# Expert weights of a mixture-of-experts stage loaded in rows twice as long, with two tiles accumulating at once

## The chip, the cores and the metric

The kernel runs on one core of one Trainium2 chip. The metric is the device time of one execution in microseconds (us), smaller being better.

## The reference

The reference is a two-layer model on 256 latent and 256 context tokens of width 1024: layer 0 has an mLSTM mixer and a dense SwiGLU, layer 1 an HGRN2 mixer and a mixture of eight SwiGLU experts of hidden width 2816, of which each latent token uses two. The change touches only the experts:

```python
def moe_swiglu(u, w_router, b_router, w_gu, w_down):
    logits = (u @ w_router).astype(F32) + b_router.astype(F32)
    top_val, top_idx = lax.top_k(logits, TOP_K)
    weights = jax.nn.softmax(top_val, axis=-1)
    combine = jnp.einsum('...k,...ke->...e', weights, jax.nn.one_hot(top_idx, N_EXPERTS, dtype=F32))
    out = jnp.zeros(u.shape[:-1] + (w_down.shape[-1],), F32)
    for e in range(N_EXPERTS):
        out = out + combine[..., e:e + 1] * swiglu(u, w_gu[e], w_down[e]).astype(F32)
    return out.astype(u.dtype)
```

`swiglu` splits `u @ w_gu` into a gate half and an up half and returns `(silu(g) * up) @ w_down`. All weights are float32: `w_gu` has 1024 rows of 5632 columns per expert, `w_down` 2816 rows of 1024.

## The kernel before, in words

The stages run one after the other; the last but one is `experts` (line 1754). It works through the eight experts in one loop whose body all engines share. For each expert the up to 128 tokens that chose it are gathered (`gather`, TensorE, into PSUM banks 4 and 5; `take`, VectorE, eight operations), multiplied with the weights, and the result is scattered back by a matmul (`scatter`, banks 6 and 7) and added to `acc` by VectorE (`add`, two operations a half).

The matmuls run in three passes, to keep float32 accuracy: each operand is split into a rounded high part and a low rest, and a product is high x high, high x low and low x high (`three_passes`, lines 1850 to 1852). The weights are split on the fly. A **unit** is one transfer into one of four ring slots (`slot`), and two **pieces** are cut from each unit; an expert has 24 units and 48 pieces. For each piece, ScalarE writes the high part (line 1939), VectorE the low part (line 2002), both into one of three piece buffers (`E_BUFS`), and TensorE multiplies with them and counts `used`. Split p waits until piece p-3 is used. A transfer waits until the low parts of both pieces of the unit four back are made (`low_done`, line 1827 issues it on SyncE's queue).

Pieces 0 to 31 belong to the up projection. Its 2816 columns per side are cut into eight tiles of 352. A unit is one tile of one side, all 1024 rows (eight chunks of 128), in rows of 352 x 4 = 1408 bytes, and its two pieces are the lower and the upper four chunks. Tile t takes pieces 4t to 4t+3: two for the gate side, two for the up side. ScalarE's `silu` follows the gate side, VectorE's `hidden` (line 2026) multiplies after the last piece. Tiles alternate between PSUM banks 0, 1 and 2, 3. The hidden rows are turned in six groups by TensorE (`turn_hidden`, after pieces 15, 19, 23, 27, 33, 35) and split again into `hid_h` and `hid_l` (line 2068).

Pieces 32 to 47 belong to the down projection. Each half of 512 output columns is made in turn: first half 0 (pieces 32 to 39) and then half 1 (40 to 47), each from four units of 6, 5, 6, 5 chunks, so pieces of 3, 3, 3, 2, 3, 3, 3, 2 chunks with rows of 2048 bytes. A half's result is weighted and split by `y_high` (line 1953) and `y_low` (line 2032) and then scattered: half 0 at pieces 39 to 43 of the same expert, half 1 in the first pieces of the next one, where both halves' work on piece buffers goes on beside it.

The engines' hand-written places are given by the piece number p in the loops of `three_passes` with `after(p)`, and of ScalarE and VectorE: in each, `split(it, p + 3)` comes first and the other work after it. The rows of the profile name lines of the kernel before; names as `resid`, `tok` and `ex` are areas used again (`e_silu` lies in `resid`, `acc` in `tok`, the raw list in `ex`).

## Time and profile before

| | |
|---|---|
| runs | 2218.1, 2219.05, 2224.69 us |
| median | 2219.05 us |
| profiled execution, span of the core | 2219.4 us |
| TensorE busy over the span | 1969.2 us (89%) |
| VectorE, ScalarE busy | 1394.1 us (63%), 1112.6 us (50%) |
| expert stage, first matmul of a weight piece to last | 1375 to 2202 us |

The page gives one number for the profiled execution, the span from the first to the last instruction of the core, 2219.4 us. The mean rate of the DMA engines over the whole span is 184 GB/s, in the expert stage it is about 335. Engines: PE is TensorE, PEld its weight loads, DVE VectorE, ACT ScalarE, SP SyncE, whose queue SPq issues the transfers. A row of order of time has the start, the duration, the engine, the line and what is written from what; in brackets stand the idle time before it and what ended it. The drawn duration of a matmul (0.32 or 0.39 us) is longer than the distance to the next, since they are pipelined.

### The profile page before, as it was taken

How to read it: one execution, taken by the hardware profiler on the slowest of the kernel's cores; microseconds unless marked ns; L12 is line 12 of the kernel's file. 1: busy time of each engine (PE TensorE's matmuls, PEld its weight loads, DVE VectorE, ACT ScalarE, POOL GpSimd, SP SyncE). 2: the span in 40 equal slices, each digit the busy share in tenths (PEclk: the TensorE clock that was granted, in tenths of full speed). 3: DMA queues.
4: the chain of work that ended last, by engine and by line, in shares of the span. 5: the costliest groups of instructions: out<-in, count | busy, mean ns of one | idle time of the engine just before them, and what ended most of it. 6: DMA issues, size and time to landing. Idle time of an engine off the chain costs nothing. (4 is left out here: it accounts for less than half of the span.)

```text
span 2219.4 us, 26725 instructions
## 1 busy us (share of the span) xinstructions
PE 1969.2 (89%) x10092; PEld 1615.5 (73%) x10092; DVE 1394.1 (63%) x1531; ACT 1112.6 (50%) x1244; POOL 110.5 (5%) x117
## 2 busy tenths in 40 slices
PE   5979988659999997869996675999999999999996
PEld 1247866548888874248895665989899898989895
DVE  5545234553233336745545844888888888888887
ACT  5433332343232225643234434677777777777765
POOL 1000012000000000000004800000000000000000
PEclk9879999879999998979998786999999999999998
DMA  9612210113232314822240004999999999999994
GB/s 328 233 60 104 76 39 1 38 38 114 76 113 76 114 57 172 310 88 94 76 152 1 1 1 149 323 348 324 345 329 348 325 348 319 354 320 336 335 331 175
DMA packets 254248, 409.11 MB, mean 184 GB/s; under 512 B 6575, under 2 KB 160327, under 8 KB 254055
## 3 DMA queue, kind: packets, MB, share of 16 engines
q1 hardware_dynamic: 254184, 408.23, 52.8%
q8 instruction: 43, 0.70, 0.1%
q14 instruction: 21, 0.17, 0.0%
HBM read 407.16 MB, written 1.05 MB: 184 GB/s over the span
## 5 line engine op out<-in xcount | busy, mean ns | idle before, releaser
L2002 DVE TENSOR_TENSOR w_low<-e_ring,w_high 128x1408 fp32r<-128x1408 f32 (+2 forms) x384 | 617.4, 1622 | 102.6 <-ACT w_high L1939 99.4
L1939 ACT ACTIVATE w_high<-e_ring 128x1408 fp32r<-128x1408 f32 (+2 forms) x384 | 528.7, 1382 | 214.7 <-PE ps L1852 212.2
L1850 PE MATMUL ps<-w_high,list_h 128*128 128x352 f32 x1024 | 338.1, 330 | 17.7 <-DVE w_low L2002 16.3
L1852 PE MATMUL ps<-w_high,list_l 128*128 128x352 f32 x1024 | 330.1, 322 | 0.0
L1851 PE MATMUL ps<-w_low,list_h 128*128 128x352 f32 x1024 | 329.3, 322 | 0.0
L1217 DVE TENSOR_TENSOR fw_low<-ring,fw_high 128x1024 fp32r<-128x1024 f32 x66 | 80.9, 1225 | 233.8 <-ACT fw_high L1183 233.8
L1850 PEld LDWEIGHTS ps<-w_high,list_h 128*128 128x128 f32 x1024 | 192.9, 188 | 26.4 <-DVE w_low L2002 25.5
L1183 ACT ACTIVATE fw_high<-ring 128x1024 fp32r<-128x1024 f32 x66 | 70.0, 1060 | 254.7 <-PE ps L1136 168.1
L1851 PEld LDWEIGHTS ps<-w_low,list_h 128*128 128x128 f32 x1024 | 193.7, 189 | 0.3
L1852 PEld LDWEIGHTS ps<-w_high,list_l 128*128 128x128 f32 x1024 | 192.9, 188 | 0.0
L1850 PE MATMUL ps<-w_high,hid_h 128*128 128x512 f32 x352 | 140.4, 399 | 5.4 <-DVE hid_l L2068 5.4
L1134 PE MATMUL ps<-u_high,fw_high 128*128 128x512 f32 x352 | 137.7, 391 | 6.7 <-DVE fw_low L1217 6.7
L1852 PE MATMUL ps<-w_high,hid_l 128*128 128x512 f32 x352 | 137.5, 391 | 0.0
L1136 PE MATMUL ps<-u_high,fw_low 128*128 128x512 f32 x352 | 137.4, 390 | 0.0
L1135 PE MATMUL ps<-u_low,fw_high 128*128 128x512 f32 x352 | 137.4, 390 | 0.0
L1851 PE MATMUL ps<-w_low,hid_h 128*128 128x512 f32 x352 | 137.3, 390 | 0.0
L387 ACT ACTIVATE u_high<-ring 128x1024 fp32r<-128x1024 f32 x96 | 98.5, 1050 | 65.7 <-PE ps L359 42.5
L419 DVE TENSOR_TENSOR u_low<-ring,u_high 128x1024 fp32r<-128x1024 f32 x96 | 111.5, 1218 | 9.5 <-ACT u_high L387 9.3
L594 DVE TENSOR_TENSOR h_part<-ring,h_part 128x1024 fp32r<-128x1024 f32 x40 | 49.0, 1225 | 79.0 <-ACT h_part L588 78.9
L588 ACT ACTIVATE h_part<-ring 128x1024 fp32r<-128x1024 f32 x40 | 42.3, 1057 | 100.9 <-PE ps L1320 100.9
L358 PE MATMUL ps<-u_high,c_parts 128*4 128x512 f32 x192 | 84.6, 441 | 6.9 <-DVE u_low L419 6.9
L359 PE MATMUL ps<-u_low,c_parts 128*4 128x512 f32 x192 | 85.0, 443 | 0.0
(323 smaller groups left out, 3631.7 us busy)
## 6 DMA issues: line engine op xcount, KB each, us to landing
e_ring<-in_e_w_gu_dram SPq DMA_DIRECT2D x128, 1408.0 KB, 8.0
ring<-in_mod_w_dram SPq DMA_DIRECT2D x24, 2048.0 KB
e_ring<-in_e_w_down_dram SPq DMA_DIRECT2D x32, 1536.0 KB, 7.2
e_ring<-in_e_w_down_dram SPq DMA_DIRECT2D x32, 1280.0 KB, 7.6
ring<-in_f_w_gu_dram SPq DMA_DIRECT2D x22, 1024.0 KB
ring<-in_h_w_in_dram SPq DMA_DIRECT2D x10, 2048.0 KB
ring<-in_m_w_in_dram SPq DMA_DIRECT2D x6, 2048.0 KB
ring<-in_f_w_down_dram SPq DMA_DIRECT2D x5, 2048.0 KB
```

The costliest lines, as they stand in the source:

```text
L358: nc.tensor.matmul(k.ps[0:4, n % 2, :], k.c_parts[:, c, :], part(k.u_high, q)[:, m, :], start=False, stop=False)
L359: last = nc.tensor.matmul(k.ps[0:4, n % 2, :], k.c_parts[:, c, :], part(k.u_low, q)[:, m, :], start=False, stop=(c == KD - 1))
L387: nc.scalar.activation(part(k.u_high, q), raw(n, q), ACT.Copy).then_inc(high_done, 1)
L419: nc.vector.tensor_tensor(part(k.u_low, q), raw(n, q), part(k.u_high, q).bitcast(F32), ALU.subtract).then_inc(low_done, 1)
L1134: nc.tensor.matmul(k.ps[:, bank, :], wh[:, m, :], k.u_high[:, m, :], start=(m == 0), stop=False)
L1135: nc.tensor.matmul(k.ps[:, bank, :], wh[:, m, :], k.u_low[:, m, :], start=False, stop=False)
L1136: last = nc.tensor.matmul(k.ps[:, bank, :], wl[:, m, :], k.u_high[:, m, :], start=False, stop=(m == KD - 1))
L1850: nc.tensor.matmul(out, high[:, f, :], w_high[:, c, :], start=(f == 0), stop=False)
L1851: nc.tensor.matmul(out, high[:, f, :], w_low[:, c, :], start=False, stop=False)
L1852: last = nc.tensor.matmul(out, low[:, f, :], w_high[:, c, :], start=False, stop=(f == total - 1))
L1939: nc.scalar.activation(piece(k.w_high, p), raw(p), ACT.Copy).then_inc(S.high_done, 1)
L2002: nc.vector.tensor_tensor(piece(k.w_low, p), raw(p), piece(k.w_high, p).bitcast(F32), ALU.subtract).then_inc(S.low_done, 1)
```

## The change

It does four things.

1. **Rows of w_gu.** A unit is now four chunks of two neighbouring tiles (704 columns, rows of 2816 bytes) of one side. Its two pieces are tile 2q and tile 2q+1 for the same four chunks. Four units make a pair of tiles: gate side lower chunks, gate side upper, up side lower, up side upper. The piece is read out of the slot with a jump from row to row.
2. **Two tiles at once.** The pieces of the two tiles alternate, so both tiles of a pair accumulate in their own banks and end one piece apart. `silu` moves to p % 8 in (2, 3), `hidden` to p % 8 in (6, 7).
3. **Rows of w_down.** A unit is up to three chunks with all 1024 columns (rows of 4096 bytes), its two pieces are the output halves 0 and 1. There are seven units of three chunks and one of one. Both halves end with the expert.
4. **The halves' results.** `y_high`, `y_low`, `scatter` and `add` of both halves now stand at the start of the next expert: scatters after pieces 3 and 6, adds at p = 4 and 7. After the last expert both are left.

The core of the diff:

```diff
@@ -44,7 +44,8 @@
 E_N = 352
 E_TILES = FFN // E_N
 E_SLOT = 6 * HALF
-E_UNITS = 2 * E_TILES + 2 * 4
+E_PAIR = 2 * E_N
+E_UNITS = 2 * E_TILES + 8
 E_BUFS = 3
 E_PIECE = 3 * HALF
...
-    down_units = [(0, 6), (6, 5), (11, 6), (17, 5)]
-    down_pieces = [x for f, m in down_units for x in ((f, 3), (f + 3, m - 3))]
+    down_units = [(f, min(3, FC - f)) for f in range(0, FC, 3)]
+    assert len(down_units) == 8 and E_TILES % 2 == 0
     def slot(j):
         return k.e_ring[:, (j % E_RING) * E_SLOT:(j % E_RING + 1) * E_SLOT]
...
-    def piece(buffer, p):
-        m, n, _ = piece_shape(p)
-        return buffer[:, (p % E_BUFS) * E_PIECE:(p % E_BUFS) * E_PIECE + m * n].rearrange("p (c n) -> p c n", c=m)
-    def raw(p):
-        m, n, first = piece_shape(p)
-        return slot(p // 2)[:, first:first + m * n].rearrange("p (c n) -> p c n", c=m)
...
-                            t, side = j // 2, j % 2
-                            src = gu[:, side * FFN + t * E_N:side * FFN + (t + 1) * E_N].rearrange("(k p) n -> p k n", p=P)
-                            dst = slot(j)[:, 0:KD * E_N].rearrange("p (k n) -> p k n", k=KD)
+                            pair, side, part = j // 4, j // 2 % 2, j % 2
+                            first = side * FFN + pair * E_PAIR
+                            src = gu[part * GS * P:(part + 1) * GS * P, first:first + E_PAIR].rearrange("(k p) n -> p k n", p=P)
+                            dst = slot(j)[:, 0:GS * E_PAIR].rearrange("p (k n) -> p k n", k=GS)
                         else:
-                            half, (f, m) = (j - Y0) // 4, down_units[(j - Y0) % 4]
-                            src = dn[f * P:(f + m) * P, half * HALF:(half + 1) * HALF].rearrange("(k p) n -> p k n", p=P)
-                            dst = slot(j)[:, 0:m * HALF].rearrange("p (k n) -> p k n", k=m)
+                            f, m = down_units[j - Y0]
+                            src = dn[f * P:(f + m) * P, :].rearrange("(k p) n -> p k n", p=P)
+                            dst = slot(j)[:, 0:m * D].rearrange("p (k n) -> p k n", k=m)
                         need = sp.snap(it * PIECES + (2 * j + 2))
...
-                pe.wait_ge(S.added, adds + 3)
...
                 with pe.Fori(0, EXPERTS) as e:
                     it = ps_ * EXPERTS + e
-                    ys = ps_ * 17 + 2 * e
-                    adds = ps_ * 34 + 4 * e
+                    ys = ps_ * 18 + 2 * e
+                    adds = ps_ * 36 + 4 * e
                     pe.wait_ge(S.list_low, ps_ * 9 + e + 1)
                     def after(p):
                         if p == 3:
-                            scatter(ys + 1, adds, 1)
+                            scatter(ys + 1, adds, 0)
+                        elif p == 6:
+                            scatter(ys + 2, adds + 2, 1)
                         elif p == 11:
                             turn_places(it, adds, e)
                         elif p == 21:
@@ -1905,27 +1906,25 @@
                             gather(ps_ * 9 + e + 1)
                         elif p in HIDDEN_TURNS:
                             turn_hidden(it, HIDDEN_TURNS.index(p))
-                        elif p == 42:
-                            pe.wait_ge(S.hid_low, it * HG + HG)
-                            scatter(ys + 2, adds + 2, 0)
-                    for t in range(E_TILES):
-                        pe.wait_ge(S.hid_done, it * E_TILES + t + 1)
-                        for side in range(2):
-                            for b in range(2):
-                                p = 4 * t + 2 * side + b
-                                three_passes(it, p, k.ps[:, 2 * (t % 2) + side, 0:E_N], k.list_h, k.list_l, b * GS, GS, KD)
-                                after(p)
+                    for j in range(Y0):
+                        pair, side, part = j // 4, j // 2 % 2, j % 2
+                        for b in range(2):
+                            if part == 0:
+                                pe.wait_ge(S.hid_done if side else S.silu_ready, it * E_TILES + 2 * pair + b + 1)
+                            three_passes(it, 2 * j + b, k.ps[:, 2 * b + side, 0:E_N], k.list_h, k.list_l, part * GS, GS, KD)
+                            after(2 * j + b)
                     pe.wait_ge(S.list_made, ps_ * 9 + e + 2)
-                    for half in range(2):
-                        for b, (f, m) in enumerate(down_pieces):
-                            if half == 0:
-                                pe.wait_ge(S.hid_low, it * HG + ((f + m - 1) // 4 + 1))
-                            p = 2 * Y0 + 8 * half + b
+                    for n, (f, m) in enumerate(down_units):
+                        pe.wait_ge(S.hid_low, it * HG + ((f + m - 1) // 4 + 1))
+                        for half in range(2):
+                            p = 2 * (Y0 + n) + half
                             three_passes(it, p, k.ps[:, 4 + half, :], k.hid_h, k.hid_l, f, m, FC)
                             after(p)
-                scatter(ps_ * 17 + 17, ps_ * 34 + 32, 1)
+                scatter(ps_ * 18 + 17, ps_ * 36 + 32, 0)
+                scatter(ps_ * 18 + 18, ps_ * 36 + 34, 1)
...
             def silu(it, t):
-                act.wait_ge(S.used, it * PIECES + (E_BUFS + 4 * t + 2))
+                act.wait_ge(S.used, it * PIECES + (E_BUFS + 8 * (t // 2) + 3 + t % 2))
                 act.wait_ge(S.hid_done, it * E_TILES + (t + 1))
...
+            act.nop().then_inc(S.silu_ready, 2)
             def y_high(pieces, half):
-                act.wait_ge(S.used, pieces + E_BUFS)
+                act.wait_ge(S.used, pieces + E_BUFS - 1 + half)
...
                     act.wait_ge(S.gathered, ps_ * 9 + e + 1)
-                    y_high(it * PIECES, 1)
+                    for half in range(2):
+                        y_high(it * PIECES, half)
...
-                        if p < 2 * Y0 and p % 4 == 1:
-                            silu(it, p // 4)
+                        if p < 2 * Y0 and p % 8 in (2, 3):
+                            silu(it, p // 8 * 2 + p % 2)
...
-                        if p == 39:
-                            act.wait_ge(S.pcopied, it + 1)
-                            y_high(it * PIECES + 40, 0)
-                y_high(ps_ * (EXPERTS * PIECES) + EXPERTS * PIECES, 1)
+                for half in range(2):
+                    y_high(ps_ * (EXPERTS * PIECES) + EXPERTS * PIECES, half)
...
             def hidden(it, t):
-                dve.wait_ge(S.used, it * PIECES + (E_BUFS + 4 * t + 4))
-                dve.wait_ge(S.silu_ready, it * E_TILES + (t + 1))
+                dve.wait_ge(S.used, it * PIECES + (E_BUFS + 8 * (t // 2) + 7 + t % 2))
+                dve.wait_ge(S.silu_ready, it * E_TILES + (t + 3))
...
-                    y_low(ys + 1, 1)
+                    for half in range(2):
+                        y_low(ys + 1 + half, half)
...
-                        if p < 2 * Y0 and p % 4 == 3:
-                            hidden(it, p // 4)
-                        if p == 4:
-                            add(adds, 1)
+                        if p < 2 * Y0 and p % 8 in (6, 7):
+                            hidden(it, p // 8 * 2 + p % 2)
+                        if p in (4, 7):
+                            add(adds + (0 if p == 4 else 2), 0 if p == 4 else 1)
...
-                        if p == 40:
-                            y_low(ys + 2, 0)
-                        if p == 43:
-                            add(adds + 2, 0)
-                y_low(ps_ * 17 + 17, 1)
-                add(ps_ * 34 + 32, 1)
+                for half in range(2):
+                    y_low(ps_ * 18 + 17 + half, half)
+                for half in range(2):
+                    add(ps_ * 36 + 32 + 2 * half, half)
```

Two places of VectorE and one of TensorE show the order. First, TensorE at the end of an expert's loop body (three matmuls a chunk; before, pieces 46 and 47 had three and two chunks, and piece 47 is the last of these rows). Before, the last two chunks:

```order
L1850 MATMUL ps<-w_high,hid_h 128x512
L1851 MATMUL ps<-w_low,hid_h 128x512
L1852 MATMUL ps<-w_high,hid_l 128x512
L1850 MATMUL ps<-w_high,hid_h 128x512
L1851 MATMUL ps<-w_low,hid_h 128x512
L1852 MATMUL ps<-w_high,hid_l 128x512
L1846 REGISTER_ALU
L1850 MATMUL ps<-w_high,hid_h 128x512
L1851 MATMUL ps<-w_low,hid_h 128x512
L1852 MATMUL ps<-w_high,hid_l 128x512
L1850 MATMUL ps<-w_high,hid_h 128x512
L1851 MATMUL ps<-w_low,hid_h 128x512
L1852 MATMUL ps<-w_high,hid_l 128x512
```

and with the change, pieces 46 and 47:

```order
L1849 MATMUL ps<-w_high,hid_h 128x512
L1850 MATMUL ps<-w_low,hid_h 128x512
L1851 MATMUL ps<-w_high,hid_l 128x512
L1845 REGISTER_ALU
L1849 MATMUL ps<-w_high,hid_h 128x512
L1850 MATMUL ps<-w_low,hid_h 128x512
L1851 MATMUL ps<-w_high,hid_l 128x512
```

The last two pieces have shrunk from fifteen matmuls to six.

Second, VectorE between split 25 and split 26 (`ex<-ps` is `take`, `e_hid` the hidden product). Before:

```order
L2002 TENSOR_TENSOR w_low<-e_ring,w_high 128x1408
L2013 ISA
L2015 TENSOR_SCALAR ex<-ps,mod_scale,mod_cols 128x128 x8
L2001 REGISTER_ALU
L2002 TENSOR_TENSOR w_low<-e_ring,w_high 128x1408
L2025 REGISTER_ALU
L2026 TENSOR_TENSOR e_hid<-resid,ps 128x352
```

and with the change:

```order
L2002 TENSOR_TENSOR w_low<-e_ring,w_high 128x1408
L2025 REGISTER_ALU
L2026 TENSOR_TENSOR e_hid<-resid,ps 128x352
L2013 ISA
L2015 TENSOR_SCALAR ex<-ps,mod_scale,mod_cols 128x128 x8
L2001 REGISTER_ALU
L2002 TENSOR_TENSOR w_low<-e_ring,w_high 128x1408
L2025 REGISTER_ALU
L2026 TENSOR_TENSOR e_hid<-resid,ps 128x352
```

Hidden product 4 now follows split 25, ahead of `take`, and product 5 follows split 26.

Third, VectorE from its hidden product 0 on (`tok<-tok,ps` is `add`). Before:

```order
L2026 TENSOR_TENSOR e_hid<-resid,ps 128x352
L2001 REGISTER_ALU
L2002 TENSOR_TENSOR w_low<-e_ring,w_high 128x1408
L2037 ISA
L2039 TENSOR_TENSOR tok<-tok,ps 128x512
L2037 REGISTER_ALU
L2039 TENSOR_TENSOR tok<-tok,ps 128x512
L2001 REGISTER_ALU
```

and with the change, from split 9's hidden product on:

```order
L2026 TENSOR_TENSOR e_hid<-resid,ps 128x352
L2001 REGISTER_ALU
L2002 TENSOR_TENSOR w_low<-e_ring,w_high 128x1408
L2025 REGISTER_ALU
L2026 TENSOR_TENSOR e_hid<-resid,ps 128x352
L2037 REGISTER_ALU
L2039 TENSOR_TENSOR tok<-tok,ps 128x512
L2037 REGISTER_ALU
L2039 TENSOR_TENSOR tok<-tok,ps 128x512
L2001 REGISTER_ALU
```

The hidden products come after splits 9 and 10, and a second pair of adds stands between split 10 and split 11.

## Rows read from the trace of the kernel before

**Rows 1.** busy time in one stretch, the fourth expert from first to next first matmul (columns as shown).
```profile
core 0: us, PE busy (x) PEld busy (x) DVE busy (x) ACT busy (x) POOL busy (x), PEclk, DMA share, GB/s
1686.36:1789.47 103.11, 101.24 (x584) 93.68 (x584) 90.69 (x79) 76.50 (x70) 0.00 (x0) 1.00 0.97 335
```

**Rows 2.** waits of that same expert: who waited for whom, us, times, longest.
```profile
ACT w_high L1939 <- PE ps L1852: 26.6, 37, 3.8
PEld ps L1850 <- DVE w_low L2002: 3.7, 5, 1.3
```

**Rows 3.** the page's list of transfers, then order of time: SyncE's issue and ScalarE's use.
```profile
e_ring<-in_e_w_gu_dram SPq DMA_DIRECT2D x128, 1408.0 KB, 8.0
...
1783.14 0.37 SPq L1827 DMA_DIRECT2D e_ring<-in_e_w_gu_dram  x1
...
1793.60 1.38 ACT L1939 ACTIVATE w_high<-e_ring 128x1408 fp32r<-128x1408 f32 x1 [0.52 <-PE ps L1852]
```

**Rows 4.** groups by line and shape, 1400 to 2150: busy us, mean ns.
```profile
L2002 DVE TENSOR_TENSOR w_low<-e_ring,w_high 128x1408 fp32r<-128x1408 f32 x237 | 381.6, 1622 | 66.1 <-ACT w_high L1939 64.4
...
L2002 DVE TENSOR_TENSOR w_low<-e_ring,w_high 128x1024 fp32r<-128x1024 f32 x28 | 34.1, 1217 | 0.0
...
L2068 DVE TENSOR_TENSOR hid_l<-ps,hid_h 128x512 fp32r<-128x512 f32 x37 | 25.3, 683 | 0.0
```

**Rows 5.** order of time where one expert ends and the next begins (start us, us).
```profile
1785.09 1.28 ACT L1939 ACT_TABLE_LOAD   x1
1786.38 1.38 ACT L1939 ACTIVATE w_high<-e_ring 128x1408 fp32r<-128x1408 f32 x1
...
1791.69 1.38 ACT L1939 ACTIVATE w_high<-e_ring 128x1408 fp32r<-128x1408 f32 x1 [0.29 <-PE ps L1852]
...
1787.80 4.86 DVE L2002 TENSOR_TENSOR w_low<-e_ring,w_high 128x1408 fp32r<-128x1408 f32 x3 [0.22 <-ACT w_high L1939]
...
1785.61 0.39 PE L1852 MATMUL ps<-w_high,hid_l 128*128 128x512 f32 x1
...
1789.01 0.39 PE L1852 MATMUL ps<-w_high,hid_l 128*128 128x512 f32 x1
1789.47 0.43 PE L1850 MATMUL ps<-w_high,list_h 128*128 128x352 f32 x1
...
1791.33 0.32 PE L1852 MATMUL ps<-w_high,list_l 128*128 128x352 f32 x1
...
1793.24 0.32 PE L1852 MATMUL ps<-w_high,list_l 128*128 128x352 f32 x1
```

**Rows 6.** order of time around piece 26 of the fourth expert, VectorE and TensorE.
```profile
1740.13 2.63 DVE L2015 TENSOR_SCALAR ex<-ps,mod_scale,mod_cols 128x128 f32<-128x128 f32 x8
1742.68 1.61 DVE L2002 TENSOR_TENSOR w_low<-e_ring,w_high 128x1408 fp32r<-128x1408 f32 x1
1744.22 0.51 DVE L2026 TENSOR_TENSOR e_hid<-resid,ps 128x352 f32<-128x352 f32 x1
...
1744.35 0.43 PE L1850 MATMUL ps<-w_high,list_h 128*128 128x352 f32 x1 [1.03 <-DVE w_low L2002]
```

**Rows 7.** order of time after the last piece of the last expert.
```profile
2201.63 0.39 PE L1852 MATMUL ps<-w_high,hid_l 128*128 128x512 f32 x1
2202.06 0.69 ACT L1953 ACTIVATE ey_high<-ps,ex 128x512 fp32r<-128x512 f32 x1 [4.37 <-PE ps L1852]
...
2204.43 1.28 DVE L2039 TENSOR_TENSOR tok<-tok,ps 128x512 f32<-128x512 f32 x2 [0.90 <-PE ps L1861]
```

**Rows 8.** line 594: duration in ns, min/median/max.
```profile
L594 DVE TENSOR_TENSOR m_part<-ring,m_part x24: 1206/1226/1227, 137.7 to 279.4; 128x1024 fp32r<-128x1024 f32 x24
```

**Rows 9.** order of time, TensorE at piece 8 of the fifth expert.
```profile
1805.66 0.32 PE L1852 MATMUL ps<-w_high,list_l 128*128 128x352 f32 x1
1806.08 0.43 PE L1850 MATMUL ps<-w_high,list_h 128*128 128x352 f32 x1
```

**Rows 10.** order of time, TensorE at piece 37 of the fourth expert.
```profile
1767.55 0.49 PE L1850 MATMUL ps<-w_high,hid_h 128*128 128x512 f32 x1 [0.67 <-DVE hid_l L2068]
```

More of the change, by code:

```diff
@@ L1778, in experts @@
     assert len(HIDDEN_TURNS) == HG
[L1781 to L1782 removed]
+    down_units = [(f, min(3, FC - f)) for f in range(0, FC, 3)]
+    assert len(down_units) == 8 and E_TILES % 2 == 0
     def slot(j):
         return k.e_ring[:, (j % E_RING) * E_SLOT:(j % E_RING + 1) * E_SLOT]
[L1787 to L1792 removed]
     def piece(buffer, p):
[L1795 removed]
+        m, n = (GS, E_N) if p < 2 * Y0 else (down_units[p // 2 - Y0][1], HALF)
         return buffer[:, (p % E_BUFS) * E_PIECE:(p % E_BUFS) * E_PIECE + m * n].rearrange("p (c n) -> p c n", c=m)
     def raw(p):
[L1799 to L1800 removed]
+        b = p % 2
+        if p < 2 * Y0:
+            return slot(p // 2)[:, 0:GS * E_PAIR].rearrange("p (c n) -> p c n", c=GS)[:, :, b * E_N:(b + 1) * E_N]
+        m = down_units[p // 2 - Y0][1]
+        return slot(p // 2)[:, 0:m * D].rearrange("p (c n) -> p c n", c=m)[:, :, b * HALF:(b + 1) * HALF]
     def passes(engine):
@@ L1865, in turn_places @@
             def turn_places(it, adds, e):
-                pe.wait_ge(S.added, adds + 3)
+                pe.wait_ge(S.added, adds + 5)
                 for i in range(2):
@@ L1956, in _ @@
             with act.Fori(0, n) as ps_:
-                act.wait_ge(S.scattered, ps_ * 34 + 1)
+                act.wait_ge(S.scattered, ps_ * 36 + 1)
                 nc.scalar.activation(k.place_cols[:, :], k.slot_no[:, :], ACT.Copy, scale=0.0)
@@ L2046, in _ @@
                     it = ps_ * EXPERTS + e
-                    ys, adds = ps_ * 17 + 2 * e, ps_ * 34 + 4 * e
+                    ys, adds = ps_ * 18 + 2 * e, ps_ * 36 + 4 * e
                     for p in range(E_BUFS):
                         split(it, p)
-                    y_low(ys + 1, 1)
+                    for half in range(2):
+                        y_low(ys + 1 + half, half)
                     for p in range(PIECES):
```

5 lines of the change are left out of this document (removed).

## The prediction

> **What bounds the kernel now.** I read the stretches first, then who waits for whom, then the order of time at the places where TensorE stands still. The change touches only the expert stage, so one expert is the unit: its 48 pieces take 103.1 us from the first matmul of one expert to that of the next, and TensorE is busy for 101.2 of them at the full clock [rows 1]. The same row has the DMA engines at a share of 0.97, VectorE at 90.7 us and ScalarE at 76.5. So two resources look full, and the question is which of them the other waits for. The list of waits answers it: ScalarE, which is the reader of what DMA brings, waited 26.6 us for TensorE to give a buffer back, and no wait for a transfer is listed at all; TensorE waited five times for VectorE's low half, 3.7 us of its weight queue [rows 2]. The DMA engines are kept busy because a transfer starts as soon as a ring slot is free, but it ends early: the transfer for pieces 4 and 5 of one expert was issued at 1783.14, a landing takes 8.0 us as the median, which is 1791.1, and ScalarE started piece 4 at 1793.60, 2.5 us later [rows 3]. **TensorE's own work bounds the stage, plus a few short stalls**, and what the transfers cost is hidden. A change of row length can pay only if it shortens those stalls; a change of order can add some.
>
> Names for the working: split p is the pair ScalarE (high) and VectorE (low) that prepares piece p; there are three piece buffers, so split p may start only when piece p-3 is used. L(p) is the start of the last matmul of piece p.
>
> **Prices.** A ScalarE copy of 1408 columns takes 1.38 us, VectorE's subtraction 1.62; one of 512 columns is taken as the 0.68 of hid_l on VectorE and a little under that on ScalarE [rows 4]. When VectorE has the next job ready it starts it 1.54 after the start of a 1408 split (1742.68 to 1744.22), so 0.08 before its end; likewise 0.43 after the start of a hidden product of 0.51, and 0.60 after the first of two adds (1.28 for two, less 0.68) [rows 5 to 7]. A piece of twelve matmuls of 352 columns costs TensorE 1.91 us (1791.33 to 1793.24, the last ones of pieces 0 and 1), so 0.16 a step. With 512 columns pieces 46 and 47 of before, fifteen matmuls, take 1789.01 - 1785.61 = 3.40, so 0.227 each. From L to ScalarE's start it takes 0.36 (1791.33 to 1791.69), after 512 columns 0.43 [rows 5, 7]. From ScalarE's end to VectorE's start 0.04, from VectorE's end to TensorE's start 0.05 [rows 5].
>
> **The transfers.** 24 units an expert remain 24, each byte is moved once as before, and the waits of SP's queue count the same pieces: unit j still waits for the slot of unit j-4. Rows twice as long can only make a transfer shorter. Value: 0 us, hidden by the 2.5 us of [rows 3]. If that cover were gone, one late landing would cost its lateness once per expert. The Trainium skill, DMA: Bandwidth & Descriptors (Why small descriptors are slow), gives a packet a fixed overhead of about 3 cycles beside its 32-byte beats; an estimate by it is 91 cycles for 2816 bytes in place of 94 for two of 1408, some 3% of transfer time. No row here prices a packet of either length by itself; by the sum above the 3% is time nobody waits for.
>
> **Reading pieces with gaps.** The splits now read runs of 352 or 512 columns with a jump between them. The trace has such reads: of the 24 operand parts of the mLSTM stage 16 read eight runs of 128 out of rows of 512, and with 1024 columns the 24 take 1206 to 1227 ns, 1226 as the median [rows 8]; contiguous ones of the expert stage take 1217 [rows 4]. Value 0 (bounds 0 and 0.01 us a split).
>
> **The end of an expert (the largest term).** The down pieces were 3,3,3,2,3,3,3,2 chunks per half; the last piece had six matmuls and the one before it nine. Now the last unit is a single chunk, so pieces 46 and 47 have three matmuls each. Split 0 of the next expert needs piece 45's buffer. Counted from L(45): 0.43 to ScalarE, 1.38, 0.04, 1.62, 0.05 give 3.52 until TensorE can start. TensorE's own work after L(45) was 16 steps of 0.227 = 3.63, enough; now it is 7 steps, 1.59. Stall: 3.52 - 1.59 = 1.93. Before, 1789.01 + 0.23 to 1789.47 was 0.23, because a 1.28 us table load held split 0 up to 1786.38 [rows 5]. That load follows split 47, which piece 44 releases; counted from L(45) it now ends at about +0.3, under the 0.43, so it adds nothing. Added: 1.70 at each of seven borders, **11.9 us**.
>
> **The start of an expert.** Both y halves are now finished here, not one: two y_high, two y_low, two scatters, two pairs of adds. TensorE's scatter is moved from after piece 42, so it costs TensorE nothing new. VectorE is the tight one. Three places:
> - Piece 3: VectorE does splits 0 to 2, then two y_low at about 0.66 apart, then split 3. It ends some 0.1 later than TensorE wants it: 0.10 (bounds 0 and 0.3).
> - The second scatter, after piece 6, waits for the first adds, which VectorE does after split 7, and split 7 waits for piece 4. From L(4): 0.36 + 1.38 + 0.04 + 1.54 + 0.60 + 0.68 + 0.05 = 4.65. TensorE gets there after two pieces and a step, 3.98: stall 0.67.
> - Piece 11: VectorE does split 10, the second hidden product, two adds, then split 11. From L(7): 0.36 + 1.38 + 0.04 + 1.54 + 0.43 + 0.60 + 0.60 + 1.62 + 0.05 = 6.62, against 0.16 + 3 x 1.91 = 5.89: 0.73.
> The stall of before at piece 8 (1805.66 + 0.16 to 1806.08, so 0.26) goes [rows 9], since the adds stand elsewhere. Together +1.24.
>
> **The middle.** Hidden product 4 moves from VectorE's place after split 22 to the place after split 25, and the transpose after piece 23 needs it. From L(22): 0.36 + 1.38 + 0.04 + 1.54 + 0.51 + 0.05 = 3.88, against 0.16 + 1.75 + 0.16 = 2.07: stall 1.81. It takes the place of the wait at piece 26 (idle 1.03 after the drawn end of a matmul, and that end lies 0.16 behind the next step: 1.19), which came from the eight list operations of 2.63 between splits 25 and 26 [rows 6]; these are then covered by the stall. Net +0.62. Queued behind the late product are the list operations and split 26, with time to spare after it (split 26 ends 0.2 before piece 26 would start).
>
> **The down part.** Each unit serves both halves, so the hidden columns are wanted at half the pace: group 4 is needed by piece 42, no more by piece 37. The wait of 0.83 there (idle 0.67 behind a drawn end 0.16 past the next step, released by hid_l) goes [rows 10], and a small fifth one at the switch of halves (0.13; of the 3.7 in [rows 2] what the other four leave). A trace of 0.08 comes at piece 38. Net -0.88.
>
> **The tail.** After the last piece both halves are left. Before: y_high at 2202.06, then y_low, scatter, and adds from 2204.43 to 2205.71, so 4.1 after the last matmul at 2201.63 [rows 7]. Now the second scatter must wait for the first adds, and the second adds for it: two adds of 1.28 and a scatter step of some 0.7 more, less the 0.6 by which the first half is ready sooner: about 5.5 after it, +1.4.
>
> **Sum**: 7 x 1.70 + 8 x (1.24 + 0.62 - 0.88) + 1.4 = 11.9 + 7.8 + 1.4 = 21.1 us. The profiled execution has a span of 2219.4, 0.35 above the median of the runs, 2219.05; so 2219.4 + 21.1 = **2240.5 us**. With border stalls of 1.5 to 1.9 above before, the rest of an expert at +0.5 to +1.6 and a tail of 1 to 1.8 this forecast reaches from 2235 to 2248.
>
> **Rivals.**
> - *Transfers did matter after all.* DMA share 0.97 speaks for it: a landing that is late now and then would look like a wait for VectorE. If longer rows and looser timing took away all stalls of an expert, 2.65 us by the places above, and the new ones did not come, it would be 2219.4 - 8 x 2.65 = 2198. Against it: in [rows 2] nothing waits for a transfer, and the five waits of TensorE have a VectorE instruction behind them. It decides where a landing comes later than the buffer. 0.06.
> - *Stalls merge.* VectorE may be ahead by more than I count, or a border stall gives it time so that those at pieces 3, 7 and 11 shrink, and the border is shorter too. The time then lies within 0.3% of before, about 2224. 0.07.
> - *Gaps in the read cost more than before.* If a split took 5% longer, VectorE would have 90.7 + 3 us of work, and every stall chain above, with two splits in it, grows by some 0.15 to 0.3, at five places an expert: 8 to 12 us more, and further ones appear: 2255. Against it stands [rows 8]. 0.09.
> - *The small last transfer.* The eighth down unit moves 512 KB where the smallest moved 1280. It keeps TensorE busy for 1.4 us where the last one did for 3.40 [rows 5]. If its transfer held the queue as long as that one's work, 3.4 us, against the 2.5 of slack, 0.9 would be missing at each of seven borders: 6 us more, 2247. The Trainium skill, DMA: Bandwidth & Descriptors (Measured), asks for at least 1 MiB a transfer, for those issued by GpSimd; its 2.0 us fixed part and bytes over 436 GB/s make an estimate of 3.2 us for this one. 0.08.
>
> **Chances.** Forecast 0.70; the rivals 0.06, 0.07, 0.09, 0.08. About 0.3% (6.7 us) is what a measurement of this kernel can tell from no change. Slower by more: 0.70 + 0.09 + 0.08 = 0.87; same 0.07; faster 0.06. The range 2229 to 2254 leaves out the first two and the far end of the third.
>
> **What would show it.** Right: the first matmul of an expert comes about 1.9 us late and is released by w_low; an expert takes some 105.8 us; TensorE waits before the second scatter, at piece 11, and before the transpose after piece 23; no wait at 26 and 37; splits of 1408 columns still take 1.62 and 1.38. Wrong: ScalarE waiting for a landing, splits that grew, or an expert of 103 us or less.

## The result, and the profile after

The changed kernel takes 2239.51 us, the median of 4 runs (2237.53 to 2244.74), against 2218.57 us for the kernel before in the same comparison (4 runs, 2215.56 to 2224.69). The ratio is 1.0096, with a 95% interval of 1.0076 to 1.0117: slower by 1%, 21 us. The forecast was 2240.5.

The stretches come first, as they did for [rows 1]. Of the changed kernel they are: the time ahead of the experts' first weight matmul, the expert stage to its last weight matmul, and what is left; then the fourth expert.

```profile
core 0: us, PE busy (x) PEld busy (x) DVE busy (x) ACT busy (x) POOL busy (x), PEclk, DMA share, GB/s
0.00:1370.21 1370.21, 1151.18 (x5417) 864.24 (x5417) 662.83 (x892) 500.38 (x688) 108.32 (x115) 0.91 0.29 99
1370.21:2215.65 845.44, 810.99 (x4672) 751.97 (x4672) 721.45 (x631) 607.93 (x550) 0.00 (x0) 1.00 0.90 321
2215.65:2235.80 20.15, 2.76 (x10) 1.35 (x8) 9.25 (x12) 5.17 (x9) 2.02 (x2) 0.71 0.13 52
...
1689.06:1794.82 105.76, 101.19 (x585) 93.70 (x585) 90.40 (x80) 76.52 (x70) 0.00 (x0) 1.00 0.91 327
```

The same stretches of the kernel before:

```profile
0.00:1375.22 1375.22, 1156.12 (x5417) 863.79 (x5417) 662.96 (x892) 500.37 (x688) 108.46 (x115) 0.91 0.28 99
1375.22:2201.63 826.41, 811.51 (x4671) 751.02 (x4672) 723.88 (x631) 607.46 (x549) 0.00 (x0) 1.00 0.95 329
2201.63:2219.40 17.77, 1.58 (x6) 0.67 (x4) 7.29 (x9) 4.75 (x8) 2.02 (x2) 0.60 0.15 59
```

The expert stage grew by 845.44 - 826.41 = 19.0 us, with TensorE's busy time the same within 0.5 and its clock at 1.00, the 2.4 GHz level, in both. So all of it is idle time of TensorE. One expert went from 103.11 [rows 1] to 105.76. What lies ahead of the experts, where the code is the same, was 5.0 us shorter in this execution, and the end 2.4 longer: the spans differ by 16.4 us while the medians differ by 20.9. Such a shift lies in the runs themselves: the 14 runs of the kernel before that accompany the first four experiments lie either at 2215.3 to 2218.1 or at 2222.5 to 2224.1, with nothing between. A span against a span is therefore worth 8 us at best here; the length of an expert is good to about 0.1, and it is what the experiments are read by.

Where the idle time is. The first view is the list of waits of the fourth expert in the changed kernel, to be held against [rows 2]:

```profile
ACT w_high L1938 <- PE ps L1851: 28.8, 38, 4.1
...
PEld ps L1849 <- DVE w_low L2002: 3.3, 3, 2.2
PE ps L1849 <- DVE w_low L2002: 2.3, 2, 1.8
...
PE ps L1885 <- DVE e_hid L2026: 1.7, 1, 1.7
...
PE ps L1860 <- DVE tok L2039: 0.5, 1, 0.5
```

TensorE's waits (PE, and PEld for its weight queue) are longer than before, all for VectorE; none is for a transfer. The order of time shows each of them. Where an expert ends and the next begins (answers to [rows 5]):

```profile
1789.68 0.63 ACT L1938 ACTIVATE w_high<-e_ring 128x512 fp32r<-128x512 f32 x1 [1.41 <-PE ps L1851]
1790.33 1.28 ACT L1938 ACT_TABLE_LOAD   x1
1791.72 3.92 ACT L1938 ACTIVATE w_high<-e_ring 128x1408 fp32r<-128x1408 f32 x3
...
1793.14 4.69 DVE L2002 TENSOR_TENSOR w_low<-e_ring,w_high 128x1408 fp32r<-128x1408 f32 x3 [2.10 <-ACT w_high L1938]
...
1791.30 0.39 PE L1851 MATMUL ps<-w_high,hid_l 128*128 128x512 f32 x1
...
1792.66 0.39 PE L1851 MATMUL ps<-w_high,hid_l 128*128 128x512 f32 x1
...
1794.82 0.43 PE L1849 MATMUL ps<-w_high,list_h 128*128 128x352 f32 x1 [1.77 <-DVE w_low L2002]
```

Piece 45 ends with the matmul of 1791.30, ScalarE starts split 0 at 1791.72, VectorE at 1793.14, and TensorE gets piece 0 at 1794.82: 3.52 us. TensorE's own work ran out at 1792.66 + 0.23 = 1792.89, so it stood for 1.93. The table load (ScalarE's row ACT_TABLE_LOAD) ended at 1791.61, 0.31 after the last use of piece 45, just ahead of the start of split 0.

The middle of the fourth expert and the start of the fifth (the first answers to [rows 6], the second to [rows 9]):

```profile
1743.58 1.63 DVE L2002 TENSOR_TENSOR w_low<-e_ring,w_high 128x1408 fp32r<-128x1408 f32 x1 [3.63 <-ACT w_high L1938]
1745.12 0.51 DVE L2026 TENSOR_TENSOR e_hid<-resid,ps 128x352 f32<-128x352 f32 x1
...
1745.55 2.64 DVE L2015 TENSOR_SCALAR ex<-ps,mod_scale,mod_cols 128x128 f32<-128x128 f32 x8
...
1745.77 0.65 PE L1885 MATMUL ps<-ident,e_hid 128*128 128x128 f32 x4 [1.74 <-DVE e_hid L2026]
...
1810.09 0.50 PE L1860 MATMUL ps<-ey_high,place_cols 128*128 128x512 f32 x1 [0.49 <-DVE tok L2039]
...
1819.51 0.43 PE L1849 MATMUL ps<-w_high,list_h 128*128 128x352 f32 x1 [0.50 <-DVE w_low L2002]
```

TensorE comes to the transposes after piece 23 and waits 1.74 for a product that VectorE makes after split 25; it waits 0.49 at the second scatter and 0.50 at piece 11. The number in brackets begins at the drawn end of the last matmul, which lies some 0.16 past the next step. After such a standstill the second matmul comes some 0.1 late as well: after the scatter's first one at 1810.09 the next starts 0.34 later, and 0.23 later where nothing waited.

The tail, answering to [rows 7]:

```profile
2215.65 0.39 PE L1851 MATMUL ps<-w_high,hid_l 128*128 128x512 f32 x1
...
2217.76 1.29 DVE L2039 TENSOR_TENSOR tok<-tok,ps 128x512 f32<-128x512 f32 x2 [0.21 <-PE ps L1860]
...
2219.10 0.50 PE L1860 MATMUL ps<-ey_high,place_cols 128*128 128x512 f32 x1 [0.91 <-DVE tok L2039]
...
2219.86 1.28 DVE L2039 TENSOR_TENSOR tok<-tok,ps 128x512 f32<-128x512 f32 x2 [0.82 <-PE ps L1860]
```

Two pairs of adds with a scatter between them: the last ends at 2221.14, 5.5 us after the last weight matmul.

The splits, by line and shape over the same stretch as [rows 4], and what the page says of queue and transfers:

```profile
L2002 DVE TENSOR_TENSOR w_low<-e_ring,w_high 128x1408 fp32r<-128x1408 f32 x229 | 367.1, 1621 | 90.8 <-ACT w_high L1938 89.8
...
L2002 DVE TENSOR_TENSOR w_low<-e_ring,w_high 128x512 fp32r<-128x512 f32 x14 | 9.6, 689 | 6.0 <-ACT w_high L1938 6.0
...
L1938 ACT ACTIVATE w_high<-e_ring 128x512 fp32r<-128x512 f32 x14 | 8.9, 633 | 13.7 <-PE ps L1851 13.7
...
q1 hardware_dynamic: 166120, 408.23, 51.6%
...
e_ring<-in_e_w_gu_dram SPq DMA_DIRECT2D x128, 1408.0 KB, 8.3
```

A split that reads runs with gaps takes 1621 ns, one that read without gaps took 1622. A transfer of 1408 KB landed 8.3 us after its issue, 8.0 before [rows 3], though its rows are twice as long.

### The profile page after: what moved, and what is told of

Same layout as the page of the kernel before. It is cut to its first block and busy times, and to the rows that moved or that the text cites. A ratio compares the mean times of both kernels' runs of the same rounds, so it can differ in the third digit from the quotient of the medians.

```text
span 2235.8 us, 26735 instructions
## 1 busy us (share of the span) xinstructions
PE 1964.9 (88%) x10096; PEld 1617.6 (72%) x10096; DVE 1393.5 (62%) x1534; ACT 1113.5 (50%) x1245; POOL 110.3 (5%) x117
## 3 DMA queue, kind: packets, MB, share of 16 engines
q1 hardware_dynamic: 166120, 408.23, 51.6%
## 5 line engine op out<-in xcount | busy, mean ns | idle before, releaser
L2002 DVE TENSOR_TENSOR w_low<-e_ring,w_high 128x1408 fp32r<-128x1408 f32 (+2 forms) x384 | 616.7, 1621 | 123.8 <-ACT w_high L1938 122.3
L1849 PE MATMUL ps<-w_high,list_h 128*128 128x352 f32 x1024 | 337.8, 330 | 24.8 <-DVE w_low L2002 24.8
L1849 PEld LDWEIGHTS ps<-w_high,list_h 128*128 128x128 f32 x1024 | 193.0, 188 | 32.4 <-DVE w_low L2002 31.4
L1849 PE MATMUL ps<-w_high,hid_h 128*128 128x512 f32 x352 | 138.7, 394 | 0.0
```

Source lines behind the costliest of these rows:

```text
L1849: nc.tensor.matmul(out, high[:, f, :], w_high[:, c, :], start=(f == 0), stop=False)
L2002: nc.vector.tensor_tensor(piece(k.w_low, p), raw(p), piece(k.w_high, p).bitcast(F32), ALU.subtract).then_inc(S.low_done, 1)
```

## The experiments

**Theory A** is the prediction's: the change is two changes, and rows and their gaps are worth nothing; the new order of release and of VectorE's work costs it all, as four stalls that can each be taken away by a line. **Theory B**: the long rows, the gaps or the single large transfer have a price or a gain of their own. Ratios are to the kernel before, run on the same chip. In the table the stalls are counted from the order of time, as the time between two starts of matmuls over that of an undisturbed step, a typical expert of each run; a dot is a stall under 0.06. The column "scatter" takes the second scatter as a whole, ahead of piece 7 or 8, and so holds the 0.1 of its late second matmul, which the other columns leave out; for the kernel before it gives the stall ahead of piece 8. The first scatter comes after piece 3, the transposes after 23 or 24.

| kernel | ratio, 95% | expert | piece 0 | 3 | scatter | 11 | transp. | others |
|---|---|---|---|---|---|---|---|---|
| before | 1 | 103.1 | 0.23 | . | 0.27 | . | . | 26: 1.18, 37: 0.83, 40: 0.13 |
| the change | 1.0096 (1.0076 to 1.0117) | 105.76 | 1.93 | 0.07 | 0.77 | 0.69 | 1.87 | 34: 0.10 |
| short rows | 1.0107 (1.0086 to 1.0128) | 105.78 | 1.93 | 0.06 | 0.77 | 0.69 | 1.86 | 34: 0.10 |
| border | 1.0078 (1.0056 to 1.0100) | 105.5 | 1.54 | 0.07 | 0.77 | 0.69 | 1.87 | 34: 0.10 |
| list and turn | 1.0060 (1.0038 to 1.0081) | 103.9 | 1.93 | 0.07 | 0.77 | 0.69 | . | 34: 0.10 |
| adds | 1.0049 (1.0028 to 1.0069) | 104.1 | 1.93 | 0.10 | . | . | 1.86 | 34: 0.10 |
| border, table | 1.0067 (1.0045 to 1.0089) | 104.4 | 0.54 | 0.07 | 0.77 | 0.69 | 1.87 | 34: 0.10 |
| all of them | 0.9930 (0.9903 to 0.9958) | 100.96 | 0.54 | 0 to 0.4 | . | . | . | 34: 0.10 |

**Short rows again, the new order kept.**

```diff
-            return slot(p // 2)[:, 0:GS * E_PAIR].rearrange("p (c n) -> p c n", c=GS)[:, :, b * E_N:(b + 1) * E_N]
+            return slot(p // 2)[:, b * GS * E_N:(b + 1) * GS * E_N].rearrange("p (c n) -> p c n", c=GS)
...
-                        sp.dma_start(dst, src).then_inc(loaded[j % E_RING], 16)
+                        for b in range(2):
+                            sp.dma_start(raw(2 * j + b), src[b]).then_inc(loaded[j % E_RING], 16)
```

Here src[b] is the half of the unit's columns that belongs to piece b, in rows of 1408 bytes, or 2048 for the down units. A piece is again contiguous in the ring, and ScalarE waits until both transfers of a unit have counted up its semaphore, 16 each.

> The changed order, but every unit comes in two transfers of half its bytes with the rows of the kernel before (1408 and 2048 bytes), and its pieces lie without gaps in the slot. Theory A (TensorE and the split chain bound the stage, transfers are hidden, gaps cost nothing): the time of the changed kernel, 2239.5 within 0.3% (2233 to 2246), an expert 105.7 us, stalls at the same pieces with the same sizes, splits of 1408 columns 1.38 and 1.62 us. Theory B (the rows of double length shorten the stage by less DMA time and hide part of the loss): slower than 2246, ScalarE waits for landings. Theory C (gaps in the pieces cost time): faster than 2233 and shorter splits.

Measured: 2243.99 us (2237.45 to 2246.20, 6 runs), and the stage from first to last weight matmul 845.53 against 845.44. One expert, the splits by shape, and the transfers:

```profile
1694.64:1800.42 105.78, 101.25 (x585) 93.80 (x585) 90.40 (x80) 76.51 (x70) 0.00 (x0) 1.00 0.93 327
```

```profile
L2001 DVE TENSOR_TENSOR w_low<-e_ring,w_high 128x1408 fp32r<-128x1408 f32 x229 | 367.0, 1621 | 90.6 <-ACT w_high L1937 89.5
```

```profile
e_ring<-in_e_w_gu_dram SPq DMA_DIRECT2D x256, 704.0 KB, 6.1
```

Every stall is there again at its size. The half of the change that its name begins with, the long rows, neither costs nor gives anything, and the gaps neither. They don't cancel each other either: the duration of a split, which shows the gaps alone, is the same. The DMA share is 0.93 here and 0.91 with long rows, at 327 GB/s both: the engines are a little less busy for the same bytes, which is of no use to anyone here. Theory B falls for the change. Length of the rows and size of a transfer are changed together here; a run further down takes them apart.

**The end of an expert.** The last down unit given two chunks instead of one:

```diff
-    down_units = [(f, min(3, FC - f)) for f in range(0, FC, 3)]
+    down_units = [(0, 3), (3, 3), (6, 3), (9, 3), (12, 3), (15, 3), (18, 2), (20, 2)]
```

> The changed kernel with down units of 3,3,3,3,3,3,2,2 chunks in place of seven of 3 and one of 1. Theory A (the stall at an expert's first piece comes from the six matmuls that are left after piece 45): the work left after piece 45 is 13 steps of 0.227 = 2.95 us in place of 1.59, so the stall at piece 0 falls from 1.93 to 0.57, an expert from 105.75 to 104.4, and the time by 7 x 1.36 = 9.5 to 2230. Rival (the stall comes from the results of both halves or from a late transfer at the border): the stall stays near 1.9 and the time at 2239.

Measured: 2234.54 us (2230.93 to 2241.90, 6 runs), stall 1.54 and not 0.57: a miss. The order of time, ScalarE's and then TensorE's, shows what I had left out, that the table load now stands behind a longer split:

```profile
1783.92 1.06 ACT L1938 ACTIVATE w_high<-e_ring 128x1024 fp32r<-128x1024 f32 x1 [0.30 <-PE ps L1851]
1785.00 1.28 ACT L1938 ACT_TABLE_LOAD   x1
1786.30 3.91 ACT L1938 ACTIVATE w_high<-e_ring 128x1408 fp32r<-128x1408 f32 x3
...
1787.63 0.40 PE L1851 MATMUL ps<-w_high,hid_l 128*128 128x512 f32 x1
```

Pieces 46 and 47 have six matmuls each, and the last of them started at 1787.63, so piece 45 was done at 1787.63 - 12 x 0.227 = 1784.9, and ScalarE could have begun split 0 0.43 later; it was in the table load until 1786.28, 0.94 too long: 0.57 + 0.94 is the stall measured, within 0.03. With the change as it stands the load ends in time by 0.1 and costs nothing; mend the border and it is next in line.

**Border and table.** A small Silu ahead of ScalarE's loop, so that the loop is entered with the table that the Silu in it needs; whether the copies run under that table too is seen by whether a load is left:

```diff
+            nc.scalar.activation(k.junk[:, 0:8], k.junk[:, 0:8], ACT.Silu)
```

> The kernel of e2 (down units 3,3,3,3,3,3,2,2) with one small Silu activation ahead of ScalarE's loop, after which the loop body holds no table load any more. e2 left a stall of 1.54 at piece 0 where 0.57 was worked out. Theory A: split 47 has 1024 columns there and ends 0.13 after the last matmul of piece 45, the table load of 1.29 behind it 1.4 after, so split 0 starts 1.0 late; without it the stall is 0.57, an expert 1.0 shorter than in e2 (105.45), so 104.45, and the time 7 us less than e2's 2234.5, so 2227.5. Rival (the stall comes from something else at the border, the loop's branch or y results): stall stays over 1.2, time over 2231.

Measured: 2232.65 us (2226.93 to 2242.18, 9 runs). No table load is left in the loop, the copies run without one, and the stall is 0.54, as the chain gives without them:

```profile
1790.94 4.15 ACT L1938 ACTIVATE w_high<-e_ring 128x1408 fp32r<-128x1408 f32 x3 [0.31 <-PE ps L1851]
```

```profile
1793.28 0.39 PE L1851 MATMUL ps<-w_high,hid_l 128*128 128x512 f32 x1
1794.04 0.43 PE L1849 MATMUL ps<-w_high,list_h 128*128 128x352 f32 x1 [0.37 <-DVE w_low L2003]
```

The expert is 1.0 shorter than with the border alone. The medians show only 2 of the 7 us that this makes, within what the intervals allow (1.0078 and 1.0067 overlap). The time alone, over 2231, would have spoken for the rival; the stall, which is what tells the two apart, fell as theory A has it.

**The product of group 4.** The list operations one split earlier, the third transposes one piece later:

```diff
-                        if p == 22:
+                        if p == 21:
...
-    HIDDEN_TURNS = (15, 19, 23, 27, 33, 35)
+    HIDDEN_TURNS = (15, 19, 24, 27, 33, 35)
```

> The changed kernel with the eight list operations one place earlier on VectorE (before split 25 in place of after it) and the third group of transposes after piece 24 in place of 23. Theory A (the stall of 1.87 before piece 24 is the chain split 25, hidden product 4, transposes): it goes, none comes at piece 26, an expert takes 1.9 less, 103.8, and the time is 8 x 1.95 = 15.6 less, 2224. Rival (the list operations or the gather of the tokens hold VectorE or TensorE anyway): a stall of over 1 us shows at piece 25 to 27, and the time stays over 2232.

Measured: 2229.93 us (2226.43 to 2238.70, 6 runs). The list of waits over four experts has no row for e_hid any more; what is left is the border and piece 11 in the first row, and the second scatter:

```profile
PE ps L1849 <- DVE w_low L2002: 9.3, 8, 1.8
...
PE ps L1860 <- DVE tok L2039: 2.0, 4, 0.5
```

The stall of 1.87 is gone whole, and nothing takes its place at pieces 25 to 27. The median came down by 9.6 us where the theory had 15.6 (2224), so the time is a miss; the stage of the profiled execution is 12.4 shorter. It would be 15.2 without the 2.8 us more of two experts, which took 105.22 and 105.35 with the same waits. In both, TensorE had just stood for the 1.93 of the border; 1.2 and 1.5 us later its matmuls of 352 columns started 0.29 apart for some 3 us and not 0.16, with a granted clock of 0.69 and 0.73 in the stretches from 1684.42 to 1690 and 1789.64 to 1796: for these 3 us it ran at the lower level, 1.2 GHz. The other experts of this run, and all but the first one of every other run, show no such drop after the border.

**The adds.** TensorE's second scatter one piece later, VectorE's second pair of adds with it:

```diff
-                        elif p == 6:
+                        elif p == 7:
...
-                        if p in (4, 7):
+                        if p in (4, 8):
```

> The changed kernel with the second scatter after piece 7 in place of 6 and the second pair of adds at p = 8 in place of 7. Theory A (the scatter waits for the first adds, piece 11 for splits 10 and 11 with a hidden product and two adds between): both stalls, 0.77 and 0.69, go, an expert takes 1.5 to 1.6 less, the time is about 12 less, 2227. Rival (VectorE has too much to do in the first twelve pieces wherever the adds stand): the stalls move to pieces 8 to 13 and the gain is under 5 us.

Measured: 2229.83 us (2224.35 to 2238.86, 9 runs). Waits over four experts: the rows for tok are gone, and of eight for w_low at L1849, as in the run above, the four at the border are left, with one at piece 3:

```profile
PE ps L1849 <- DVE w_low L2002: 8.9, 5, 1.8
PE ps L1885 <- DVE e_hid L2026: 6.9, 4, 1.7
```

Both stalls, 0.77 and 0.69, went with one move: the 1.28 of adds no longer stand in the same three-piece window as the second hidden product.

**All together**, with long rows, and the same with short rows:

> The changed kernel with all mendings: down units 3,3,3,3,3,3,2,2, no table load in the loop, list operations one place earlier, third transposes after piece 24, second scatter after piece 7, second adds at p = 8. Theory A (the terms are independent and transfers stay hidden): stalls of an expert fall from 5.0 to about 0.7, an expert takes 105.75 - 1.36 - 1.95 - 1.6 = 100.9 us, the time is 2202, which is 0.7% faster than the kernel before. Rival (at this pace the transfers bind, 34.6 MB in 100.9 us being 343 GB/s): TensorE waits behind ScalarE that waits for landings, an expert takes 102 to 103, the time is 2210 to 2218.

> The kernel of e6 with the short rows of e1 (1408 and 2048 bytes, two transfers a unit, pieces without gaps). If long rows are worth something once TensorE has few stalls, this is slower than e6 by over 3 us and its landings come later than ScalarE's buffers; if row length is worth nothing here, the same within 3 us.

Measured: 2202.65 us (2199.82 to 2208.89, 6 runs), ratio 0.9930; with short rows 2202.22 (2198.54 to 2207.78, 6 runs), ratio 0.9928 (0.9902 to 0.9955). An expert of each:

```profile
1681.40:1782.36 100.96, 100.58 (x585) 93.85 (x585) 90.47 (x80) 73.86 (x67) 0.00 (x0) 1.00 0.94 342
```

```profile
1677.04:1778.00 100.96, 100.58 (x584) 93.86 (x584) 90.47 (x80) 74.17 (x68) 0.00 (x0) 1.00 0.97 343
```

The expert is 4.8 shorter than the change's; 8 x 4.8 = 38.4, and the medians differ by 36.9. By the drawn durations TensorE is busy for all but 0.4 us. Here the transfers come into view for the first time, in the run with long rows and one transfer a unit, and not with short rows and two. Over four experts:

```profile
ACT w_high L1938 <- DMA e_ring<-in_e_w_gu_dram: 1.1, 4, 0.7
```

In the whole stage ScalarE waited for a landing in six of the eight experts (the expectation that follows says seven), 2.3 us in all, and TensorE lost 0.3 us for it at piece 3 in three of them.

**Long rows, two transfers a unit.** Either the long rows or the single transfer of 1408 KB could be what is late there. Everything of the last kernel is kept, and each unit is cut in two along its chunks, so that rows stay long:

```diff
-                        sp.dma_start(dst, src).then_inc(loaded[j % E_RING], 16)
+                        sp.dma_start(dst[:, 0:half], src[:, 0:half]).then_inc(loaded[j % E_RING], 16)
+                        sp.dma_start(dst[:, half:], src[:, half:]).then_inc(loaded[j % E_RING], 16)
```

> The kernel of e6 (long rows) with every unit in two transfers, of one half of its chunks each, as e7 has two, but rows of 2816 and 4096 bytes kept. In e6 ScalarE waited for a landing at piece 2 of seven of eight experts and TensorE lost 0.3 us at piece 3 in three of them; in e7 it lost none. If the number of transfers made that difference, this one loses none either and an expert takes 100.96 us; if the short rows made it, piece 3 waits again in some experts, as in e6 (101.0 to 101.3). The time is 2202 within 3 us under either.

Measured: 2207.18 us (2200.09 to 2210.57, 6 runs) beside a before of 2220.80, ratio 0.9937 (0.9918 to 0.9956); the expert 100.94, and no wait for a transfer:

```profile
1681.69:1782.63 100.94, 100.59 (x585) 93.81 (x585) 90.45 (x80) 74.18 (x68) 0.00 (x0) 1.00 0.94 342
```

A half landed 6.3 us after its issue, with rows of either length, the whole one 8.4. So it is the size of a transfer that uses up the slack of 2.5 [rows 3], not its rows, as far as one profiled execution of each kernel tells; in the time of the kernel the three can't be told apart.

**Is the new order worth anything?** The kernel before with two of the same lines, the list operations one split earlier and no table load in the loop:

```diff
+            nc.scalar.activation(k.junk[:, 0:8], k.junk[:, 0:8], ACT.Silu)
...
-                        if p == 22:
+                        if p == 21:
```

> The kernel before, with its own rows and order, with two of the mendings: list operations one place earlier on VectorE, and no table load in the loop. Theory A: the stall of 1.19 at piece 26 and the restart of 0.1 go, that of 0.23 at piece 0 too, so an expert takes 101.5 us in place of 103.1 and the time is 2217.4 - 8 x 1.3 - 7 x 0.3 = 2205. Rival (transfers with short rows, busy at 0.96 before, bind): an expert of 102.5 or more, time over 2211, ScalarE waits for landings.

Measured: 2206.65 us (2202.35 to 2209.19, 9 runs), ratio 0.9945 (0.9927 to 0.9963), expert 101.6, with the stalls 0.29 at piece 8, 0.85 at 37 and 0.13 at 40 left; at piece 0 there is none. The stall at 37 should go if the two parts of the next expert's list are made later, the high one by ScalarE and the low one by VectorE:

```diff
-                        if p == 32:
+                        if p == 37:
...
-                        if p == 33:
+                        if p == 38:
```

> The kernel of e8 (rows and order of before, list operations early, no table load in the loop) with the token list's split moved back as well: its high part on ScalarE from p = 32 to 37, its low part on VectorE from p = 33 to 38. Theory A (the wait of 0.85 at piece 37 for hid_l is VectorE being held by the list's subtraction of 1.2 ahead of it): it goes, the expert falls from 101.64 to 100.8, the time from 2206.6 by 8 x 0.85 = 7 to 2200. Rival (VectorE has no room later either): a stall of 0.5 or more shows at pieces 38 to 44 and the time stays over 2204.

Measured: 2209.57 us (2208.83 to 2221.38, 12 runs), ratio 0.9965 (0.9950 to 0.9979), expert 102.3, longer by 0.7: a miss. The waits of TensorE over four experts:

```profile
PE ps L1850 <- DVE w_low L2004: 1.8, 4, 0.5
PE ps L1850 <- DVE hid_l L2070: 1.6, 4, 0.4
```

The stall at 37 went only from 0.85 to 0.55, and two came, 0.14 at 41 and 0.61 at 42. The order of time (fourth expert) has the reasons. The part of `hid_l` that piece 37 needs starts at 1762.00, right behind split 37, and that split (1760.32) began only after VectorE had waited 0.75 for ScalarE: the subtraction of 1.22 that was moved away had mostly filled this wait. In its new place (1770.70) it holds up split 42, and the list's high part on ScalarE holds up split 41. So this one move does not gain anything; other places were not tried. In the order of the change both halves share a unit and the products are wanted at half the pace, and neither 37 nor 40 waits. With all its mendings it is ahead of the kernel before with these two by 0.65 us an expert; the two ratios, 0.9930 and 0.9945, have intervals that overlap.

## Why the prediction was right

The time, 2240.5 against 2239.5, is right by its own steps, and they can be held one by one against what was measured.

- **Transfers 0, gaps 0.** Shown, by the short rows in the new order (105.78 against 105.76 an expert, splits of 1621 ns in both). The Trainium skill, DMA: Bandwidth & Descriptors (Why small descriptors are slow), gives each packet a fixed overhead, from which the prediction estimated some 3% of the transfer time. The trace agrees in size: the share fell from 0.93 to 0.91 between short and long rows at 327 GB/s, and from 0.97 to 0.94 at 343 and 342 GB/s with all mendings. But the landing of 1408 KB came no sooner (8.3 against 8.0), though the prediction had that long rows "can only make a transfer shorter", and ScalarE never waited for it.
- **The border, 1.93.** Measured 1.93 (0.23 before), and the table load ended 0.31 after the last use of piece 45, as reckoned. That the stall is the chain of one release was shown by lengthening TensorE's work in it, only in two steps: I had not seen that the load, free here, is the next bound.
- **The start.** Piece 3: 0.07 against 0.10. The scatter started 0.65 late against 0.67; its adds end at 1810.04 (1808.76 + 1.28) and it starts at 1810.09, the 0.05 of the chain. The 0.77 of the table holds 0.1 more, the late second matmul after a standstill, which no chain of the prediction counted. Piece 11: 0.69 against 0.73. Together with the 0.27 gone at piece 8 that is +1.26, forecast +1.24.
- **The middle.** 1.87 against 1.81; the stall of 1.18 at piece 26 is gone, covered as said.
- **The down part.** No stall at 37 and 40. The small stall of 0.08 was put at 38; it is 0.10 and at 34. The prediction took the 0.13 of the switch of halves for what the other four stalls leave of the 3.7 of [rows 2]; they leave 1.2, so the 0.13 does not follow from there, but the order of time has it at piece 40 (0.13).
- **The tail.** 5.5 us after the last matmul, as forecast. A further 1.0 us in the last stretch is the last store, which ended 4.0 after VectorE's last operation and not 3.1; nothing in the change bears on it.

The stage grew by 19.0 where 11.9 + 7.8 = 19.7 were forecast, the first expert by 2.4 and not 2.7 (107.33 against 104.92), the next six by 15.7 and not 16.1, the last by 0.9 and not 1.0. The sum was made on the span of one execution, 2219.4; on the 2218.57 that the kernel before took beside the changed one it gives 2239.7. That the median came out within 1 us is luck in part: the stages ahead of the experts alone differ by 5 us from one execution to another.

**The rivals.** *Transfers matter* falls: no wait for one in the change. They first show in a kernel faster by 37 us, where TensorE lost 0.3 us for them in three of eight experts. *Stalls merge*: they did not, each was removed by itself without changing another by more than 0.1. *Gaps*: 1621 ns against 1622. (Its price was summed wrong: 0.15 to 0.3 at five places of eight experts is 6 to 12 us, not 8 to 12.) *The small last transfer*: with 512 KB nothing waited at the border for a landing, split 0 started 0.42 after the release. The Trainium skill, DMA: Bandwidth & Descriptors (Measured), asks for 1 MiB a transfer, for those that GpSimd issues. For SyncE's, in this stage, going below it cost nothing: with long rows two transfers of 704 KB had the DMA share of 0.94 at 342 GB/s that one of 1408 had, and they left more slack.

## What to carry to other kernels

With few buffers between engines that hand work on, count for each place how long the chain from the last use of a buffer to the next use takes, and hold it against the work that the last engine still has: that gave every large stall of this change within 0.1 us before it ran. A shorter last piece, or one more operation on the tight engine in such a window, costs whatever part of it exceeds the slack, and moving the operation by one piece can give it all back. Look at a bandwidth share near 1 only after the waits: here it was 0.97 while nobody waited for a transfer, and longer rows had no one to help.

## What the runs showed of the hardware that I had not expected

- Two table loads of 1.28 us sat in every pass of ScalarE's loop, though copies and Silu can run under one table; one small Silu ahead of the loop took both away (from 70 to 68 instructions an expert, 76.5 to 74.2 us busy). In the kernel before, one of them held up the border by 0.23; without them and with the list operations one split earlier that kernel is 0.55% faster.
- Doubling the rows (1408 to 2816 bytes, and 2048 to 4096) took a third of the packets away (254184 to 166120 on the queue) and left share of the queue (52.8 to 51.6%) and landing (8.0 to 8.3 us) nearly where they were.
- In the full queue of this stage a transfer of half the bytes does not land in half the time: 6.1 to 6.3 us from issue to landing for 704 KB, 8.0 to 8.4 for 1408.
- After TensorE has stood, its second matmul comes late too: 0.26 us behind the first and not 0.16 with 352 columns (1794.82, 1795.08), 0.33 and not 0.23 with 512. So it is after the stalls at pieces 0 and 11 and at the scatter, and at 26 and 37 of the kernel before.
- A standstill of 1.93 us can be followed by some 3 us at the lower clock level, which cost 1.4 us; it was so after two of the seven borders of one run and after none in the other runs with that stall. What decides it is not shown.
